# Attention with stacked keys, paired heads and a sink column, and recurrent steps that begin after three of a head's five tiles

## The reference

```python
def gla_chunk_step(state, q, v, k, g):
    # S_t = diag(exp g_t) S_{t-1} + k_t v_t^T, o_t = S_t^T q_t over one chunk
    ...

def sink_attend(q, keys, vals, sink, mask):
    logits = jnp.einsum('bqgrd,bkgd->bgrqk', q, keys).astype(F32) * (AT_HD ** -0.5)
    if mask is not None:
        logits = jnp.where(mask, logits, -jnp.inf)
    s = sink.astype(F32)[None, :, :, None]
    m = jnp.maximum(jnp.max(logits, axis=-1), s)
    p = jnp.exp(logits - m[..., None])
    denom = jnp.sum(p, axis=-1) + jnp.exp(s - m)
    o = jnp.einsum('bgrqk,bkgd->bqgrd', p / denom[..., None], vals.astype(F32))
    return o.astype(q.dtype)
```

## Time and profile before

| | |
|---|---|
| median of 3 runs | 2097.64 us |
| lowest, highest | 2085.96, 2100.85 us |
| the profiled execution: time, span | 2097.79 us, 2096.0 us |
| PE busy | 1961.0 us (94%) |
| DVE busy | 1192.7 us (57%) |
| ACT busy | 690.3 us (33%) |
| POOL busy | 22.4 us (1%) |
| chain that ended last, by engine | PE 78%, DVE 14%, ACT 4%, DMA 2%, issue 2% |
| DMA share, rate | 23.7% of 16 engines, 78 GB/s read |

### The profile page before, as it was taken

One profiled execution on the slowest core, in us unless ns is written; L12 is line 12 of the kernel. 1 busy time (PEld: TensorE's weight loads), 2 busy tenths in 40 slices (PEclk: granted clock), 3 DMA queues, 4 the chain that ended last, 5 costly groups with the idle time before them and its releaser, 6 DMA issues.

```text
span 2096.0 us, 25879 instructions
## 1 busy us (share of the span) xinstructions
PE 1961.0 (94%) x10776; PEld 1640.8 (78%) x10776; DVE 1192.7 (57%) x2032; ACT 690.3 (33%) x1049; POOL 22.4 (1%) x18
## 2 busy tenths in 40 slices
PE   4999999999889899999999998899899889999997
PEld 2999999999878688888888887665665767777875
DVE  2555556555764666336542664755454478477485
ACT  3333333333222333113321332355154334133232
POOL 0000000000300000000000000000000000000000
PEclk9999999999999899999999999889989999999998
DMA  6221222112202133323332322100100212232332
GB/s 268 91 78 44 81 81 81 61 61 81 71 1 61 51 121 111 100 93 119 121 101 93 109 91 94 51 11 1 51 10 1 79 62 91 81 99 81 91 93 98
DMA packets 45333, 165.82 MB, mean 79 GB/s; under 512 B 4897, under 2 KB 5281, under 8 KB 45089
## 3 DMA queue, kind: packets, MB, share of 16 engines
q1 hardware_dynamic: 45216, 164.16, 23.7%
HBM read 162.05 MB, written 2.10 MB: 78 GB/s over the span
## 4 chain that ended last, share of the span: by engine, by line
PE 78%; DVE 14%; ACT 4%; DMA 2%; issue 2%; SPq 0%; DVEq 0%
PE slot L375 20%; PE slot L377 19%; PE slot L376 19%; DVE ACC L1375 6%; PE MA L510 4%; PE slot L704 3%; DVE WL L1059 3%; PE MB L428 3%; PE slot L695 2%; ACT WH L769 1%; DMA WR<-in_w 1%; PE MB L461 1%; PE MB L421 1%; DVE ACC L1383 1%; DMA ada_raw<-in_ada 1%
## 5 line engine op out<-in xcount | busy, mean ns | idle before, releaser
L375 PE MATMUL slot<-HH,WH 128*128 128x256 f32 (+2 forms) x2016 | 726.3, 360 | 44.5 <-DVE HL L1157 16.9
L376 PE MATMUL slot<-HL,WH 128*128 128x256 f32 (+2 forms) x2016 | 708.7, 352 | 0.0
L377 PE MATMUL slot<-HH,WL 128*128 128x256 f32 (+2 forms) x2016 | 708.3, 351 | 0.0
L375 PEld LDWEIGHTS slot<-HH,WH 128*128 128x128 f32 x2016 | 384.9, 191 | 125.4 <-issue 76.8
L376 PEld LDWEIGHTS slot<-HL,WH 128*128 128x128 f32 x2016 | 385.1, 191 | 38.1 <-issue 2.2
L377 PEld LDWEIGHTS slot<-HH,WL 128*128 128x128 f32 x2016 | 384.1, 191 | 38.5
L1059 DVE TENSOR_TENSOR WL<-WR,WH 128x1024 fp32r<-128x1024 f32 x204 | 249.3, 1223 | 246.0 <-ACT WH L769 244.4
L769 ACT ACTIVATE WH<-WR 128x1024 fp32r<-128x1024 f32 x204 | 215.4, 1057 | 368.2 <-DMA WR<-in_w 368.1
L1375 DVE SCALAR_TENSOR_TENSOR ACC<-UP,cw,ACC 128x512 f32<-128x512 f32 x352 | 263.9, 750 | 8.6
L375 PE MATMUL slot<-GH,WH 128*128 128x512 f32 (+1 forms) x528 | 192.3, 364 | 8.4 <-DVE GL L1388 8.4
L377 PE MATMUL slot<-GH,WL 128*128 128x512 f32 (+1 forms) x528 | 190.9, 362 | 0.0
(11 more groups left out here) (177 smaller groups left out, 1837.7 us busy)
## 6 DMA issues: line engine op xcount, KB each, us to landing
WR<-in_w SPq DMA_DIRECT2D x204, 512.0 KB, 3.6
ada_raw<-in_ada SPq DMA_DIRECT2D x84, 512.0 KB, 4.6
AD<-in_ada SPq DMA_DIRECT2D x3, 2048.0 KB, 23.2
X<-in_x SPq DMA_DIRECT2D x1, 3072.0 KB, 11.9
out<-Y SPq DMA_DIRECT2D x8, 256.0 KB, 2.2
Y<-in_masks SPq DMA_DIRECT2D x1, 512.0 KB, 19.7
...
```

Of the source, the lines that this page charges most:

```text
L375: mm(SLOT[s][:, po], WH[w % NB][:, k, :], hi[:, k, to], start=(k == 0), stop=False)
L376: mm(SLOT[s][:, po], WH[w % NB][:, k, :], lo[:, k, to], start=False, stop=False)
L377: last = mm(SLOT[s][:, po], WL[w % NB][:, k, :], hi[:, k, to], start=False, stop=(k == kn - 1))
```

## The change

In the recurrence three tiles instead of five stand ahead of the first step. A step projects the values and gate of its own head and then the decays and query of the next one. The last step therefore has two tiles of its own; the output products of the heads that are done begin at its sixth place, and two of them lie between the last head's key-value products, outputs and sums. `gate` on VectorE stands behind level 0. The adaLN pieces' loads are tied to tiles two earlier.

In the attention a key tile is kept twice as `KS[0]` and `KS[1]`, with 64 rows of high parts of one key head and 64 rows of its low parts; a query's high part stands in both halves of `QH[half]`, its low part in both of `QO[half]`. So two products of 128 rows replace three of 64. ScalarE makes the high copies, four per query tile, and VectorE the four subtractions. The sink's logit is a column that PE writes behind the scores, by a product of ones with the sink over 128, so that the maximum and the exponential's sum include it. Units alternate between the two key heads, and the values of two units are issued together, one key head's on the upper 64 output rows and the other's on the lower. GpSimd scales the probabilities.

```diff
-            KH = sb("KH", [P, TOK], F32R, s)
-            KO = sb("KO", [P, TOK], F32R, s)
-            QH = sb("QH", [P, 4, LAT], F32R, s)
-            QO = sb("QO", [P, 4, LAT], F32R, s)
+            KS = [sb(f"KS{i}", [P, TOK], F32R, s) for i in range(2)]
+            QH = [sb(f"QH{i}", [P, 4, LAT], F32R, s) for i in range(2)]
+            QO = [sb(f"QO{i}", [P, 4, LAT], F32R, s) for i in range(2)]
...
+            PB = [sb(f"PB{i}", [P, 5 * P + 2], F32, s) for i in range(3)]
+            PX = sb("PX", [P, 5 * P], F32, s)
...
+        PT = [t[:, :, :].rearrange("p f o -> p (f o)")[:, 0:5 * P] for t in AR[1:4]] + [PX[:, :]]
...
-        UNITS = [(bi, half, r) for bi in range(LAT // P) for half in range(2) for r in range(4)]
+        UNITS = [(bi, half, r) for bi in range(LAT // P) for r in range(4) for half in range(2)]
...
-            after, n, t = {}, 4 * ADA_FIRST, 5
-            for h in range(HEADS - 1):
+            after, n, t = {}, 4 * ADA_FIRST, 3
+            for h in range(HEADS):
                 after[t + 1], after[t + 2] = 2, 2
                 t += 5
-            after[t + 1], after[t + 2] = 2, 2
...
+            for i in range(2):
+                for u in range(len(UNITS)):
+                    n = 2 + window(UNITS[u][0])[1]
+                    pool.wait_ge(rden_ready, i * len(UNITS) + u + 1)
+                    pool.tensor_scalar(PB[u % 3][:, 0:n * P], PB[u % 3][:, 0:n * P], rden[u % 4][:, :], None, ALU.mult).then_inc(probs_scaled, 1)
...
-                    if project:
+                    if project or n < 4:
                         s = (parity + n // 2) % 2
                         if n % 2 == 0:
                             begin_tile(s)
                         half_tile(s, n % 2, HH, HL, hg=True)
-                    elif 2 <= n < HEADS + 1:
-                        pe.wait_ge(early_lo, n - 1)
-                        head_products(n - 2)
+                    if not project and n == 5:
+                        for s in range(2):
+                            begin_tile(s)
+                    if not project and n >= 5:
+                        head_products(n - 5)
                     between(n)
 
             def head_products(k):
...
+                if k < HEADS - 1:
+                    pe.wait_ge(early_lo, k + 1)
...
-            for j in range(3, 5):
-                full_tile(j % 2, TOK, HH, HL, hg=True)
             head_step(0, 1, tail=False)
 
             for _ in range(3):
                 head_step(1, 0)
                 head_step(0, 1)
-            for s in range(2):
-                pe.wait_ge(evacuated[s], T_HGO // 2)
-            for s in range(2):
-                begin_tile(s)
             head_step(1, 0, project=False)
             key_value(1)
+            head_products(HEADS - 3)
             outputs(1)
+            head_products(HEADS - 2)
...
+            def at_score(u, i, bi, half, r):
+                hd = slice(i * 8 + half * 4 + r, i * 8 + half * 4 + r + 1)
                 S = (MB, MA)[u % 2]
                 first, n = window(bi)
                 if u >= 2:
                     pe.wait_ge(probs_ready, unit.times(1, (u - 1)))
                 q = slice(bi * P, (bi + 1) * P)
-                parts_of = [(QH, KH), (QH, KO), (QO, KH)]
-                for e, (a, b) in enumerate(parts_of):
-                    mm(S[:, PC0:PL0], a[hp, r, q], b[hp, 0:CTX], start=(e == 0), stop=(e == 2))
+                for e, a in enumerate((QH, QO)):
+                    mm(S[:, PC0:PL0], a[half][:, r, q], KS[half][:, 0:CTX], start=(e == 0), stop=(e == 1))
                 edges = ([(0, 0)] if bi > 0 else []) + ([(n - 1, 1)] if bi < LAT // P - 1 else [])
-                for e, (a, b) in enumerate(parts_of):
-                    mm(S[:, PL0:PL0 + n * P], a[hp, r, q], b[hp, CTX + first * P:CTX + (first + n) * P], start=(e == 0), stop=False)
+                for e, a in enumerate((QH, QO)):
+                    mm(S[:, PL0:PL0 + n * P], a[half][:, r, q], KS[half][:, CTX + first * P:CTX + (first + n) * P], start=(e == 0), stop=False)
                 for e, (at, which) in enumerate(edges):
-                    last = mm(S[:, PL0 + at * P:PL0 + (at + 1) * P], tri[:, 2, :], tri[:, which, :], start=False, stop=(e == len(edges) - 1))
-                last.then_inc(at_scores, 1)
+                    mm(S[:, PL0 + at * P:PL0 + (at + 1) * P], tri[:, 2, :], tri[:, which, :], start=False, stop=(e == len(edges) - 1))
+                end = PL0 + n * P
+                mm(S[:, end:end + 1], ones[:, :].to_broadcast([P, P]), sink8[:, hd], start=True, stop=True).then_inc(at_scores, 1)
...
-            def at_values(v, bi, half):
+            def at_values(v):
+                bi, _, r = UNITS[2 * v]
                 first, n = window(bi)
-                pe.wait_ge(pt_ready, unit.times(1, (4 * v + 4)))
-                if half == 0 and bi > 0:
-                    pe.wait_ge(at_out, block_n.times(1, bi))
+                pe.wait_ge(pt_ready, unit.times(1, (2 * v + 2)))
+                if r == 0 and bi > 1:
+                    pe.wait_ge(at_out, block_n.times(1, bi - 1))
+                o = bi % 2 * 512 + r * P
                 for j, c in enumerate([0, 1] + [CCH + first + j for j in range(n)]):
-                    last = mm(SLOT[1][64 * half:64 * half + 64, 0:512], AV[:, c, 64 * half:64 * half + 64],
-                              PT[v % 2][:, j, :, :].rearrange("p r q -> p (r q)"), start=(j == 0), stop=(j == n + 1))
+                    for half in range(2):
+                        last = mm(SLOT[1][64 * half:64 * half + 64, o:o + P], AV[:, c, 64 * half:64 * half + 64],
+                                  PT[(2 * v + half) % 4][:, j * P:(j + 1) * P], start=(j == 0), stop=(j == n + 1))
...
-                at_score(0, *UNITS[0])
                 pe.wait_ge(roped, rot.now())
-                at_score(1, *UNITS[1])
+                at_score(0, i, *UNITS[0])
+                at_score(1, i, *UNITS[1])
...
                 for u in range(len(UNITS)):
                     if u + 3 < len(UNITS):
-                        at_score(u + 3, *UNITS[u + 3])
-                    if u % 4 == 0 and u:
-                        at_values(u // 4 - 1, *UNITS[u - 1][:2])
+                        at_score(u + 3, i, *UNITS[u + 3])
                     at_turn(u, *UNITS[u])
-                at_values(7, *UNITS[-1][:2])
+                    if u % 2 == 0 and u:
+                        at_values(u // 2 - 1)
+                at_values(len(UNITS) // 2 - 1)
...
+                for t in (5 * h, 5 * h + 1):
+                    act.wait_ge(evacuated[t % 2], t // 2 + 1)
                 mix_keys(b, 0)
-                if project:
-                    split_high(tile.now() + AHEAD)
+                split_high(tile.now() + AHEAD)
                 if tail:
                     key_copies()
                     output_copies()
-                if project:
-                    decays(1 - b, FORE, s)
+                values(s)
                 if tail:
                     token_std(1.0 / P, 0, MB)
-                if project:
-                    decays(1 - b, BACK, 1 - s)
+                gate(1 - s, h)
                 mix_keys(b, 1)
                 head.add()
                 value_copy(b)
                 mix_keys(b, 2)
                 if project:
-                    query(s, h + 1)
+                    decays(1 - b, FORE, s)
+                else:
+                    split_high(tile.now() + AHEAD)
                 mix_keys(b, 3)
                 mix_keys(b, 4)
                 if project:
-                    values(1 - s)
+                    decays(1 - b, BACK, 1 - s)
                 mix_keys(b, 5)
                 if project:
                     split_high(tile.now() + AHEAD)
@@ -909,7 +917,7 @@
                 scores.add()
                 ada_copy()
                 if project:
-                    gate(s, h + 1)
+                    query(s, h + 1)
 
...
+                go(PB[u % 3][:, 0:n * P + 1], (MB, MA)[u % 2][:, PC0:PC0 + n * P + 1], ACT.Exp, scale=AT_SCALE, bias=nm[u % 2][:, :],
+                   accum_out=den[u % 4][:, :]).then_inc(probs_ready, 1)
...
+                def key_parts():
+                    his.add()
+                    act.wait_ge(raw_roped, his.now())
+                    for half in range(2):
+                        h = slice(64 * half, 64 * half + 64)
+                        go(KS[half][h, 0:CTX], AVT[h, 0:CTX], ACT.Copy)
+                        last = go(KS[half][h, CTX:TOK], RAW[0][h, :], ACT.Copy)
+                    last.then_inc(hi_copied, 1)
...
+                def query_parts(r):
+                    his.add()
+                    act.wait_ge(raw_roped, his.now())
+                    for half in range(2):
+                        for to in (64 * half, 64 - 64 * half):
+                            last = go(QH[half][to:to + 64, r, :], RAW[(r + 1) % 2][64 * half:64 * half + 64, :], ACT.Copy)
+                    last.then_inc(hi_copied, 1)
                 next_tile()
```

(39 more changed lines are left out.)

94 lines of the change are left out of this document (36 added, 58 removed).

## The result

The changed kernel takes 2129.07 us (median of 4 runs, 2126.16 to 2131.3) against 2099.24 us of the kernel before: ratio 1.0155, 95% interval 1.0111 to 1.0199. It is slower by 1.5%, where 2092 us and no change that can be told were forecast.

A forecast was written before the change was run, and what follows sets the result against it. TensorE was taken to set the recurrent steps with projections and the attention loop, with VectorE in the last step's chain. 2097.79 - 9.4 (recurrence) + 20.2 (rope) - 16.4 (loop, clock included) = 2092.2 us; range 2066 to 2130.

The forecast's parts named there:

- GpSimd's scaling: Attention loop: GpSimd scales 640 columns of probabilities in 0.70 us, up to 1.5 beside a busy VectorE.
- The latency term: Attention loop: 2.27 us from the end of scores until the next even unit's transposes may start, within a 5.3 us pair.
- The loop's sum: Attention loop: 84.3 us per key tile at full clock against 103.6 before; gain counted at 38 for both key tiles.
- the tiling rule: Loop scores: dropping switches between 64-row scores and full transposes would save some 0.2 us per unit, 13 in all; not counted.
- all eight short pairs: First block of both loops: half clock makes each short pair 7.2 us, 2.7 more than 4.55, 21.6 for eight.
- the clock hardly falls: Rival on the attention loops: TensorE's clock hardly falls or returns within a pair; 2070 us, chance 0.20.
- the clock stays low: Rival on the attention loops: clock low throughout, up to 2172 us; 2121 with about eight long pairs low; chance 0.15.
- the pairs overlap only in part: Recurrence's last step: VectorE products clash with GpSimd's split of finished heads, 0 to 0.64 us for four per level; 3 taken.
- the earlier step start gives nothing, since the last step grows by all 16.8: Rival on the recurrence: the last step gives back the whole earlier start; 2101 us, chance 0.08.
- a serial chain of three engines: Attention rope: rotation, ScalarE copies, VectorE subtractions in series, 7.95 us per link against 6.35; sum +20.2, bounds +5 and +26.
- The rival of cheap half-height copies: Rival on the rope: half-height copies cheaper than full ones, rope stays near TensorE's pitch; 2077 us, chance 0.10.
- The rivals on the values and the clock: Loop rivals: values on two output halves don't overlap (2124 us, 0.07); clock high (2070, 0.20); clock low for long (0.15).

The follow-up runs named there:

- e9: The changed kernel with GpSimd's scaling written as two operations (times the reciprocal, plus 0.0) instead of one: 2081.07 us, ratio 0.9917 to the kernel before.
- e4: The changed kernel with probability scaling on VectorE and ScalarE splitting the next weight tile before the last query tile's copies: 2064.58 us.
- e2: The changed kernel with the scaling of the probabilities back on VectorE instead of GpSimd: 2074.06 us, 0.9882 of the kernel before.
- e3: The changed kernel without GpSimd's subtraction for the low parts of the seven finished heads (output products read older ones): 2116.62 us.
- e1: The kernel before with only the recurrence's part of the change, attention as before: 2095.61 us, ratio 0.9985.

## Why the prediction was wrong

**GpSimd's scaling, the term that decides.** The prediction took 0.70 us for 640 columns, bound 1.5, by the earlier trace rows. It is 1.88. The row was of the right engine and the right opcode, but of a form with two operations, and the change's has one; the page prints both as TENSOR_SCALAR. The latency term carries it once per pair: 1.2 us by 32 pairs is 38 us. Between the changed kernel and e9, which differ in this form alone, the loops differ by 44.5 us and the times by 48. The granted clock is higher in e9's loops too (0.91 and 0.97 against 0.88 and 0.84), and the runs don't separate this part. The prediction named GpSimd as what would make it wrong, "over 1.3 us, which adds 0.6 to each of 32 pairs"; the trigger was right, but its bound stopped at 1.5. That 2129 still lies within the stated 2066 to 2130 is luck: the range was widened for a clock that stays low, not for this.

**The loop's sum otherwise.** Near GpSimd's assumed length it was about right, somewhat too long: 84.3 at full clock, against 83.5 and 80.4 in e9, whose loops did not have the full clock throughout. Within it the values at 1.2 us were right (1.24 from their start to the next scores in e4), and the scores 0.1 too long: 1.12 against 1.02. So half of the gain that the tiling rule promised and that was left out, 0.2 us per unit, is there. It lies ahead of the triangle masks: they start 0.26 us after the last score product in the kernel before (1425.00 to 1425.26) and 0.18 in e4.

**The clock.** 21.6 us were added for the first block of both loops. In e9 the two loops together are 164 us where 84.3 twice and 21.6 make 190: most of this cost wasn't there. The fall itself was: the first 10 us of the changed kernel's first loop had a granted clock of 0.50, those of e2's loops 0.76 and 0.52. But it was over behind them in e2, at 4.1 us for both loops, and in e4 it didn't come. So the step that failed is the length, all eight short pairs. Of the rivals "the clock hardly falls" was nearer; "the clock stays low" was wrong, although its 2121 lies near the result: with GpSimd out of the loop (e4) the same products run at 1.00, and the changed kernel's 0.91 in mid-loop stands beside PE's waits for GpSimd.

**The recurrence.** The start 16.8 us earlier is there (15.5 at the last step's diagonal scores, 15.5 to 20.2 over all runs). Counted back were 7.4 us, of which 3 for the clash with GpSimd. The last step grew by 15.1 (63.8 for 48.7), of which 8.7 go with GpSimd's subtractions (e3); the other 6.4 stand for the remaining 4.4. The step that failed is "the pairs overlap only in part", with 0.64 us for some of the products by the one row of 1.19. What stood beside that row was a copy of GpSimd, 1.21 us long, not a subtraction:

```profile
588.33 1.21 POOL L348 TENSOR_SCALAR HH<-Y 128x768 fp32r<-128x768 f32 x1 [10.07 <-DVE Y L1290]
```

Beside a subtraction of 1.82 us, which started at 559.69, the same trace of before has such a product at 560.05 with 1.87 us. In these rows a product waits out the whole of what it meets, and in the changed kernel GpSimd's fourteen instructions, 22 us in all, lie in a row beside the products that the levels wait for. The rival "the earlier step start gives nothing, since the last step grows by all 16.8" is what happened (e1: 2095.6 us, the step 16.9 longer); it had 0.08 of the chance.

**The rope.** The mechanism, a serial chain of three engines with the weight split behind the last copies, was right, down to VectorE's last wait (3.71 us). The size was short: links of 8.7 to 9.7 instead of 7.95 (whose parts add up to 7.92, as those of the 20.2 do to 20.4). Four copies took 2.56 for 2.2, four subtractions 2.79 for 2.5, the wait for the rotation 1.28 for 1.06 and a handover, and in the longest links PE came back from its idle time at the lower clock: the rotation at 1368.11 took 1.60 us instead of 1.02, with 0.50 granted behind it. So it was 29.8 us, outside the bounds of +5 to +26. Of the 9.6 us over, 6.4 are the six links between queries, above all because copies and subtractions of 64 partitions in a row took longer than those of 128 in the earlier trace rows: 0.64 us each for 0.53, and 0.69 for 0.61. Why, no run tells. The rival of cheap half-height copies (2077) is excluded by these.

**The sum.** 2092.2, with 6.9 for the recurrence (7.7 for the last step and 1.3 for its start, less the 2.1 that are not its own), 9.6 for the rope and 19.2 for the loop, is 2127.9; the result is 2129.1. The loop's 19.2 are the 44.5 between the changed kernel and e9, less 26.3 for the clock and the rest, and 1.0 because the gain was counted at 38 where the loops of before, 205.6 us, less 168.6 are 37.0. The rivals on the values and the clock, which took 0.42 of the chance, were of less weight than one duration whose bound had one sentence. What stays open is why GpSimd is slower with one operation than with two; the runs show that it is, for immediate and column.
